# A hybrid encoder layer on one NeuronCore: input projections as products of split operands, and eight modulation sums moved to the solve stage

## The reference

```
sh1, sc1, g1, sh2, sc2, g2 = split(mod, 6)
h  = rms_norm(x, norm1) * (1 + sc1) + sh1
zp = h @ w_in                                 # 512 x 1024 by 1024 x 2824
z_rwkv, z_pool, z_fox = columns 0:1024, 1024:1280, 1280:2824 of zp
mixed = concat(rwkv7(z_rwkv), pool(z_pool), forgetting_attention(z_fox))
x  = x + g1 * (mixed @ w_out)
h  = rms_norm(x, norm2) * (1 + sc2) + sh2
x  = x + g2 * moe(h)                          # 4 of 32 experts, clamped SwiGLU
out = rms_norm(x, norm_f)
```

## Time and profile before

| | |
|---|---|
| time, median of 3 runs | 1626.63 us (1625.39 to 1629.79) |
| profiled execution: its own time, its span | 1626.56 us, 1624.6 us |
| projections, first `rw` to the end of `v` 3 and its `ada` | 38.2 to 211.8 us of the span |
| of these: `q` 3 ends, `lora` and `kkn`, `k` 0 begins, `f` ends | 124.2, to 130.7, 180.7 us |
| solve and attention (first `MP` to last `GH`) | 221.7 to 321 us |
| output projection, router | 328 to 426 us |
| experts and end | 426 us to the end |

### The profile page before, as it was taken

The page is one execution under the profiler, slowest core; times in us unless marked ns, Lnnn a source line. Parts: engine busy times, 40 slices in busy tenths (PEclk is TensorE's granted clock), DMA queues, the critical chain, the costliest instruction groups (busy, mean ns, idle before and its releaser), DMA issues.

```text
span 1624.6 us, 22048 instructions
## 1 busy us (share of the span) xinstructions
PE 1542.7 (95%) x8260; PEld 1163.2 (72%) x8260; DVE 1341.9 (83%) x1048; ACT 979.2 (60%) x787; POOL 187.9 (12%) x210
## 2 busy tenths in 40 slices
PE   3999989998699999999999999999999999999996
PEld 2444358845567787888888888888888888888873
DVE  5557447474878999999999999999999999999987
ACT  4013233311546776777777777777777777777772
POOL 1000121000001110100000100000110000010051
PEclk9999999998789999999999999999999999999998
DMA  9686020242369998999999999999999999999993
GB/s 377 254 343 236 29 91 29 69 168 110 143 258 347 339 390 335 381 388 390 388 380 383 381 380 387 396 391 376 387 379 387 386 395 385 377 388 377 375 379 123
DMA packets 85761, 506.81 MB, mean 312 GB/s; under 512 B 11008, under 2 KB 12336, under 8 KB 33360
## 3 DMA queue, kind: packets, MB, share of 16 engines
q1 hardware_dynamic: 70880, 453.85, 71.5%
q0 software_dynamic: 9104, 34.08, 5.8%
q10 hardware_dynamic: 5728, 18.18, 2.8%
HBM read 477.25 MB, written 28.84 MB: 312 GB/s over the span
## 4 chain that ended last, share of the span: by engine, by line
PE 87%; DVE 7%; DMA 2%; issue 2%; ACT 1%; POOL 1%; SPq 0%; DVEq 0%; POOLq 0%
PE ps L2067 61%; PE ps L1218 8%; PE ps L2083 2%; PE ps L1991 2%; PE ps L1295 2%; PE ps L1120 2%; PE ps L1224 2%; DVE w_lo L1474 2%; PE ps L2046 2%; DMA Wt<-in_ada_w 2%; PE ps L2056 1%; PE ps L1166 1%; PE ps L1193 1%; PE ps L1185 1%; PE ps L2089 0%
## 5 line engine op out<-in xcount | busy, mean ns | idle before, releaser
L1474 DVE TENSOR_TENSOR w_lo<-w_raw,w_hi 128x2048 fp32r<-128x2048 f32 x384 | 864.9, 2287 | 72.5 <-ACT w_hi L1468 72.4
L1468 ACT ACTIVATE w_hi<-w_raw 128x2048 fp32r<-128x2048 f32 x384 | 736.6, 1920 | 291.0 <-PE ps L2067 291.0
L2067 PE MATMUL ps<-w_hi,xTh 128*128 128x512 f32 x1024 | 408.3, 399 | 6.4 <-DVE w_lo L1474 5.8
L2067 PE MATMUL ps<-w_lo,xTh 128*128 128x512 f32 x1024 | 401.6, 392 | 0.0
L2067 PE MATMUL ps<-w_hi,xTl 128*128 128x512 f32 x1024 | 275.7, 391 | 0.0
L2067 PEld LDWEIGHTS ps<-w_hi,xTh 128*128 128x128 f32 x1024 | 194.6, 190 | 60.0 <-issue 16.5
L2067 PEld LDWEIGHTS ps<-w_hi,xTl 128*128 128x128 f32 x1024 | 193.4, 189 | 40.4
L2067 PEld LDWEIGHTS ps<-w_lo,xTh 128*128 128x128 f32 x1024 | 194.3, 190 | 38.5
L2067 PE MATMUL ps<-w_hi,aTh 128*128 128x512 f32 x512 | 202.4, 395 | 0.0
L2067 PE MATMUL ps<-w_lo,aTh 128*128 128x512 f32 x512 | 199.4, 389 | 0.0
L2067 PE MATMUL ps<-w_hi,aTl 128*128 128x512 f32 x512 | 157.6, 389 | 0.0
(11 more groups left out here) (396 smaller groups left out, 1372.3 us busy)
## 6 DMA issues: line engine op xcount, KB each, us to landing
w_raw<-in_moe_w_gu SPq DMA_DIRECT2D x256, 1024.0 KB, 6.6
w_raw<-in_moe_w_down SPq DMA_DIRECT2D x128, 1024.0 KB, 7.0
Wt<-in_ada_w SPq DMA_DIRECT2D x19, 1024.0 KB, 10.4
y_rows<-R ACTq DMA_DIRECT2D x30, 512.0 KB, 6.7
Wt<-in_w_in SPq DMA_DIRECT2D x5, 2048.0 KB, 13.4
y_rows<-Wt POOLq DMA_DIRECT2D x1, 8704.0 KB, 40.7
R<-in_ada_w SPq DMA_DIRECT2D x5, 1024.0 KB, 8.2
R<-in_x SPq DMA_DIRECT2D x2, 2048.0 KB, 10.3
```

Source lines behind the costliest of these rows:

```text
L1468: nc.scalar.activation(w_hi[:, at[-1] % HI_SLOTS, :], w_raw[:, at[-1] % RAW_SLOTS, :], ACT.Copy).then_inc(hi_rdy, 1)
L1474: nc.vector.tensor_tensor(w_lo[:, s, :], w_raw[:, s, :], w_hi[:, at[-1] % HI_SLOTS, :].bitcast(F32), ALU.subtract).then_inc(lo_rdy, 1)
L2067: ins = mm(ps[:, bank0 + c, :], x[:, k, :], w[:, 512 * (banks * i + c):512 * (banks * i + c) + 512], start=(first and i == 0 and x is xh a ...
```

## The change

The projections are computed from split operands. `hT` is split into `hTh` (rounded, ACT) and `hTl` (rest, DVE, in place of `hT`), once. The weights are split 128 columns at a time: ACT writes the rounded part of 8 x 128 columns to one of four slots `blk_hi`, DVE writes the rest in place (`blk_lo` is the memory of `blk`). A new step `sp` i does that for split i, two jobs ahead of the job that needs it; the first four are made before the steps. A projection job is then 24 float32r matmuls in place of 8 in float32. `v` 0 is computed in four parts of 128 columns, each as soon as its split is there; `v` 1 to 3 in one. `f` is padded to 128 columns by zeros.

The eight `acc` steps 8 to 15 become 16 passes of 128 x 1024, with two buffers `late_part` loaded by SP 512 KB at a time, and stand between `M` 1,1 and the last level of the solve, one after every second step; their four `ada` jobs stand behind `W` 0 to 3. Because `hTh` lies where the window sums go, POOL starts these only after `v` 3, and DVE finishes the pooled means at `trBK` 2; the `pm` jobs move behind `trBK` 3. The reload of `x` moves behind the last `ada`. The zeroing of output rows is laid out anew, and its wait on ACT moves from `GH` to `f`. Some semaphores are merged.

```diff
     for n in range(8):
-        steps += [("rw", n)] + acc(n)
-    steps += [("q", 0)] + turned(ADA_FIRST)
-    for n in range(4):
-        steps += ([("q", n)] if n else []) + acc(8 + n)
+        steps += product("rw", n) + (acc(n - 1) if n else [])
+    steps += product("q", 0) + acc(7) + product("q", 1) + turned(ADA_FIRST) + product("q", 2) + product("q", 3)
     steps += [("lora", n) for n in range(6)]
     steps += [("kkn", ct) for ct in range(CT)]
     for n in range(4):
-        steps += [("k", n)] + acc(12 + n)
+        steps += product("k", n)
     steps += [("rk", ct) for ct in range(CT)]
-    steps += [("pz", 0), ("pz", 1), ("f", 0)]
-    for t in range(TT):
-        steps += [("v", t), ("ada", ADA_FIRST + 4 + t)]
+    steps += product("pz", 0) + product("pz", 1)
+    steps += [("sp", SPLIT[("v", 0)]), ("sp", SPLIT[("v", 1)]), ("f", 0), ("sp", SPLIT[("v", 2)])]
+    steps += [("v", t) for t in range(TT)]
...
-    steps += [("trAV", t) for t in range(TT)] + [("pm", 0)] + [("trBK", t) for t in range(TT)] + [("pm", 1)]
+    steps += [("trAV", t) for t in range(TT)] + [("trBK", t) for t in range(TT)] + [("pm", 0), ("pm", 1)]
...
+    ada_at = solve.index(("W", 0))
     for n, s in enumerate(solve):
         steps.append(s)
+        if 6 <= n < 6 + 2 * 2 * KT and n % 2:
+            steps.append(("acc", KT + (n - 6) // 4, (n - 6) // 2 % 2))
+        if ada_at <= n < ada_at + 4:
+            steps.append(("ada", ADA_FIRST + 4 + n - ada_at))
...
+            job_done(pool, ("v", TT - 1))
             for ct in range(CT):
                 read_by(pool, ("pz", ct))
...
+            def high(i):
+                key, c = split_of(i)
+                if i >= SPLIT_SLOTS:
+                    job_done(act, SPLITS[i - SPLIT_SLOTS])
+                if SPLITS[i] == ("f", 0):
+                    act.wait_ge(pool_chain, pf_zero[0])
+                blk_ready(act, key)
+                s.activation(blk_hi[:, i % SPLIT_SLOTS, :, :], blk[BLK_OF[key] % 2][:, :, c:c + P], ACT.Copy
+                             ).then_inc(part_hi, 1)
+            act.wait_ge(ada1_sum, 1)
+            high(0)
+            high(1)
             act.wait_ge(modc_rdy, 1)
...
+            for k in range(KT):
+                act.wait_ge(h_act if k % 2 else h_dve, k // 2 + 1)
+                s.activation(hTh[:, k, :], hT[:, k, :], ACT.Copy).then_inc(part_hi, 1)
+            for i in range(2, AHEAD):
+                high(i)
...
+            def low(i):
+                key, c = split_of(i)
+                n = BLK_OF[key] % 2
+                dve.wait_ge(part_hi, split_count(i))
+                v.tensor_tensor(blk_lo[n][:, :, c:c + P], blk[n][:, :, c:c + P],
+                                blk_hi[:, i % SPLIT_SLOTS, :, :].bitcast(F32), ALU.subtract).then_inc(part_lo, 1)
+            low(0)
+            low(1)
+            for k in range(KT):
+                dve.wait_ge(part_hi, 2 + k + 1)
+                v.tensor_tensor(hTl[:, k, :], hT[:, k, :], hTh[:, k, :].bitcast(F32), ALU.subtract).then_inc(part_lo, 1)
+            for i in range(2, AHEAD):
+                low(i)
...
                     for k in range(KT):
                         if step == ("rw", 0):
-                            pe.wait_ge(h_act if k % 2 else h_dve, k // 2 + 1)
-                        ins = mm(b[0:rows, :], w[:, k, c:c + rows], hT[:, k, :], start=(k == 0), stop=(k == KT - 1))
+                            pe.wait_ge(part_lo, 2 + k + 1)
+                        mm(b, wh[:, k, :], hTh[:, k, :], start=(k == 0), stop=False)
+                        mm(b, wl[:, k, :], hTh[:, k, :], start=False, stop=False)
+                        ins = mm(b, wh[:, k, :], hTl[:, k, :], start=False, stop=(k == KT - 1))
                 elif kind == "v":
...
-                    for k in range(KT):
-                        ins = mm(b, hT[:, k, P * t:P * t + P], w[:, k, :], start=(k == 0), stop=(k == KT - 1))
+                    for part in (((3,), (0,), (1,), (2,)) if t == 0 else ((0, 1, 2, 3),)):
+                        lo, hi = part[0], part[-1] + 1
+                        o = b[:, P * lo:P * hi]
+                        oc = o.rearrange("p (c n) -> p c n", n=P)
+                        pe.wait_ge(part_lo, split_count(SPLIT[("v", part[-1] if t == 0 else 2)]))
+                        for k in range(KT):
+                            mm(oc, hTh[:, k, ts], blk_hi[:, lo:hi, k, :], start=(k == 0), stop=False)
+                            mm(o, hTh[:, k, ts], wl[:, k, P * lo:P * hi], start=False, stop=False)
+                            ins = mm(oc, hTl[:, k, ts], blk_hi[:, lo:hi, k, :], start=False, stop=(k == KT - 1))
```

More of the change, by code:

```diff
@@ L134 @@
 STEPS = plan()
-JOBS = [s for s in STEPS if s[0] not in ("fox", "acc")]
+JOBS = [s for s in STEPS if s[0] not in ("fox", "acc", "sp")]
 JOB = {s: n for n, s in enumerate(JOBS)}
@@ L216, in build @@
         R0 = early.enter_context(nc.sbuf_tensor("R0", [P, LATE], F32))
+        rounded = ExitStack()
+        blk_lo = [rounded.enter_context(nc.sbuf_tensor(f"blk_lo{n}", [P, KT, 512], F32R)) for n in range(2)]
+        hTh = rounded.enter_context(nc.sbuf_tensor("hTh", [P, KT, S], F32R))
+        blk_hi = rounded.enter_context(nc.sbuf_tensor("blk_hi", [P, SPLIT_SLOTS, KT, P], F32R))
+        rounded.close()
         Wt = early.enter_context(nc.sbuf_tensor("Wt", [P, 24576], F32))
@@ L339, in build @@
         late_in = [sem(f"late_in{s}") for s in range(3)]
+        late2_in = [sem(f"late2_in{s}") for s in range(2)]
         ada_acc = sem("ada_acc")
@@ L734, in _ @@
                     continue
-                if kind == "acc" or "A" not in READERS[kind]:
+                if kind == "sp":
+                    high(step[1])
+                if kind in ("acc", "sp") or "A" not in READERS[kind]:
                     continue
@@ L1004, in _ @@
                         v.tensor_tensor(Kh[:, ct, :], kT[:, ct, :], Kh[:, ct, :], ALU.mult).then_inc(elem_dve, 1)
+                if step == ("trBK", 2):
+                    for ct in range(CT):
+                        dve.wait_ge(pool_sum, ct + 1)
+                        for h in range(2):
+                            hs = slice(HD * h, HD * h + HD)
+                            tt = win[ct][h][hs, :]
+                            link(v.tensor_tensor(fix[hs, :], tt[:, PAD:2 * PAD], rcnt[hs, ct, :], ALU.mult))
+                            link(v.tensor_tensor(fix[hs, :], fix[hs, :], pz[hs, ct, PAD:2 * PAD], ALU.subtract))
+                            link(v.scalar_tensor_tensor(out=tt[:, PAD:PAD + S], in0=tt[:, PAD:PAD + S],
+                                                        scalar=1.0 / POOL_WINDOWS[2 * ct + h],
+                                                        in1=pz[hs, ct, PAD:PAD + S], op0=ALU.mult, op1=ALU.subtract))
+                            last = v.tensor_copy(tt[:, PAD:2 * PAD], fix[hs, :])
+                            if h == 0:
+                                link(last)
+                        last.then_inc(pooled, 1)
                 if "D" not in READERS[kind]:
@@ L1150, in _ @@
                 kind = step[0]
-                if kind == "acc":
+                if kind in ("acc", "sp"):
                     continue
@@ L1628, in _ @@
             s_.activation(gm, gm, ACT.Exp).then_inc(gexp_rdy, 1)
-            s_.activation(sat[:], sat[:], ACT.Sigmoid, scale=ALPHA).then_inc(sat_rdy, 1)
+            s_.activation(sat[:], sat[:], ACT.Sigmoid, scale=ALPHA).then_inc(gexp_rdy, 1)
             xt_evac(0, 0)
@@ L1662, in _ @@
             act.wait_ge(tail_mm, 1)
-            s_.activation(tailT, ps[:, 4:6, :], ACT.Copy).then_inc(tail_ev, 1)
+            s_.activation(tailT, ps[:, 4:6, :], ACT.Copy).then_inc(gmt_rdy, 1)
             sigmoid(E - 1, place(E - 1, KT - 1))
```

150 lines of the change are left out of this document (88 added, 62 removed).

## The result

The changed kernel takes 1666.5 us, the median of 4 runs (1660.09 to 1672.41), beside 1627.82 us (1625.39 to 1629.79) of the kernel before on the same chip: 1.0239 times as long, interval 1.0219 to 1.0259. I had forecast 1626.5 us, 1616 to 1637. It is slower, and outside the range.

The account below looks back on a forecast made before the run. PE was taken to bound the projections, and DVE in a loop with PE the solve. From 1626.6 us: - 14.5 (to `v` 3) + 1.5 (to `MP`) + 1.0 (restart) + 3.4 (`ada`) + 8.5 (sums) = 1626.5, range 1616 to 1637.

Parts of the forecast that it names:

- the gain of 14.5 us to the end of `v` 3: Projections: `v` 3 ends at 197.3 against 211.8, of which 3.5 us are only the `ada` jobs moved away.
- Prices: A job of 24 products 5.45 us; a split's halves 1.22 and 1.04; the 16 half sums 19.0 us of DVE.
- Start: First projection: `rw` 0 starts 4.3 us late, at 42.5, and loses 1.7 us to half clock.
- `rw` and `q`: `q` 3 ends at 115.1 instead of 124.2, 9.1 us gained; split 8 hidden, 2.0 us wait ahead of `ada`.
- `lora` to `k`: `k` 2 waits 6.3 us for split 14, then 1.7 of half clock; `k` 3 ends at 151.4, before 158.3.
- `v`: Split 22 and the parts of `v` 0 come together; `v` 0 ends at 181.0, `v` 3 at 197.3.
- To the first `MP`: From `v` 3 to `MP` 11.3 us, before 9.8: loss 1.5; DVE finishes the second mean in 2.7.
- Solve: Late sums expose 8.5 us (bounds 4 and 19); the four `ada` jobs add 3.4.
- the term of the clock: Ahead of the solve: 1.0 us (0 to 1.7) for a slower restart after PE idles some 3 us.
- the falling clock in the solve: Sign that the prediction is wrong: the clock column falls in the solve; no size given.
- a DVE that is full: Sign in the solve: DVE busy over 90% in 230 to 290 us.
- DVE becomes the bound: Rival, in the solve: all 19.0 us of late sums exposed, 1626.5 + 10.5 = 1637 us; chance 0.29.

Follow-up runs that it names:

- e3: Changed kernel with the zeroing of output rows issued after `q` 3 instead of after `rw` 7: 1654.87 us, 1.0171 of the kernel before.
- e4: Changed kernel with split 14 (for `k` 2) made ahead of `q` 3: 1651.57 us, 1.0168 of the kernel before.
- e5: Changed kernel with 41 matmuls of constants put where PE stands idle: 1660.54 us, 1.0205 of the kernel before.
- e6: Changed kernel with DVE's finish of the pooled means and the `pm` jobs behind the solve's first level: 1656.17 us, 1.0192 of the kernel before.
- e1: Kernel before, float32 projections kept, with the late sums in the solve and their four `ada` jobs at its end: 1646.99 us, ratio 1.0132.
- e2: Changed kernel without the late sums, their loads and their four `ada` jobs: 1650.13 us, 1.0127 of the kernel before.
- e9: e8 with the pooled windows moved so that POOL's sums and DVE's finish run beside the `v` products: 1617.60 us, 0.9937 of the kernel before.
- e8: Changed kernel with e3, e4, e6 and the late sums as eight whole rows in the `v` stage: 1631.75 us, 1.0020 of the kernel before.
- e10: Changed kernel with e3 and e4 together: 1649.85 us, 1.0124 of the kernel before.

## Why the prediction was wrong

The direction of each term was right: products gain, waits in the projections and sums in the solve give it back. What failed is that the gain of 14.5 us to the end of `v` 3 was nothing, and that three costs were missing or far too small: the zeroing transfer beside the loads, DVE's finish of the means ahead of the first `MP`, and the slow clock around the waits. On the marks of the table the misses add up to the whole difference: 13.7 us to the end of `v` 3 (steps 3 to 5), 6.0, 12.6 and 2.3.

1. **Prices: right.** A job of 24 products takes 5.55 us (forecast 5.45), a split's halves 1.22 and 1.05 us (1.22 and 1.04), the products of 128 columns 0.111 us at full clock (0.12). The Trainium skill's 81 ns ("TensorE: Matmul & The Clock Gate", Back-to-back issue gap) is lower than what this trace shows.
2. **Start: right.** `rw` 0 at 43.38 (42.5), half clock until 46.
3. **`rw` and `q`: failed, 8.8 us.** `q` 3 ended at 123.9, not 115.1: 0.9 from the start, 1.2 from 12 jobs of 5.55 us, 1.8 for split 8 (forecast as hidden), 3.0 because PE waited 5.0 us ahead of the `ada` jobs and not 2.0, and 1.9 because these then ran at a lower clock (5.37 us, not 3.5). I took the loads by their durations of before, and had no zeroing transfer in the sum. It ran beside the `k` block before, too (DMA share 1.01 in 110 to 124 us), but behind it in order of issue, and the block landed in 13.2 us, not 25.9. e3 shows that the zeroing makes up 5.0 of the 8.8.
4. **`lora` to `k`: right.** `k` 2 waited 5.9 us (6.3) for split 14; with the half clock behind it, it cost 6.7 us by e4 (8.0). To the start of `v` 0 another 0.9 us was lost.
5. **`v`: failed, 4.0 us.** 0.8 us of waiting for split 22, which by the sum came together with the parts, and then half clock into `v` 1. The stretch took 31.8 us in each run with split products but e5 (33.4). That the clock makes it so long is read from the table; no run removed the wait.
6. **To the first `MP`: failed, 6.0 us (17.3 instead of 11.3).** POOL's sums took 7.0 us (7.1), but I let DVE finish the first mean beside them and start the rest at their end. In the order of steps the finish stands behind the second `trBK` copy. It began 3.6 us later and did both means (5.3 us instead of 2.7). e6 gets 6.4 us back.
7. **Solve: the term of the clock, 9.9 us instead of 1.0.** The sums' exposed time was 10.2 us (8.5 forecast, and 4 to 19 as bounds); DVE needed 21.4 us for the 16 half sums (19.0), 1361 ns in place of 1260 for each of the 14 two-input passes. The stretch with the `ada` jobs grew by 5.4 us (3.4); they take 1.06 us each there, not 0.86. What I had priced far too low is the slow clock in the solve: 4.9 us more between `T` and `W` and 5.0 ahead of `T`, where I had 1.0 for one restart. The 5.0 hang on the idle time ahead of `MP`: e1, with `MP` 10.7 us behind `v` 3, has none of them, and e5, which fills the idle time, has 2.1. The 4.9 do not follow from DVE's waits one by one: behind five of them the clock was 0.98 to 1.00. Most of the 4.9 stand at the wait for POOL. The sums alone bring them (e1), and so in part does the changed kernel without the sums (e2, 2.8 us). Why that stretch is 13 us long and not 7 is open.

Of the signs that I had named, the falling clock in the solve came, and a DVE that is full did not: it was busy 43.0 of the 60 us from 230 to 290 (72%, forecast over 90%). PE's idle time came from single sums that stood ahead of a normalisation, not from a lack of DVE time.

The rival "DVE becomes the bound" names DVE's part of this and allows for slow clock behind stalls, but its price, 10.5 us, was that of the sums alone. And its 1637 still had the 14.5 us of gain in it, of which nothing arrived.

Left open: the 2.3 us at the end, where the code is the same and the other kernels differ by up to 6 us (1296.3 to 1302.5), and why the clock differs between executions of the same kernel.

## What to carry to other kernels

When PE gets faster, everything that was hidden behind it is priced again: for each step, list the transfers and the other engines' blocks that fall in the same window, those that the change doesn't touch too (before, PE had no wait behind the zeroing; after, it cost 5 us). Put a term for the clock beside each new wait of PE, with a wide range: here it went from nothing to several times the wait. Read the clock stretch by stretch before you say which wait it belongs to. Work that an engine has to do once belongs where that engine idles and its inputs are ready: the same sums cost 15 us between `T` and `W` (e1) and next to nothing beside `v` (e9), where DVE had had over 20 us to spare, once memory had been found for them.

## What the runs showed of the hardware

- In the changed kernel 12 of the 14 two-input passes of the late sums took DVE 1.27 us, and two that began during a product of POOL took 1.59 and 2.17. Which began first mattered: four passes that began just ahead of such a product kept their 1.27 us, and the product took 1.7 to 2.1 us in place of 1.26. In e9 both engines' rows stretch each other. The timeline of DVE and then of POOL: two low halves took 3.51 us where the same two took 2.36 in e8, and POOL's sums 1.9 to 2.0 us instead of 1.06.

```profile
162.81 3.51 DVE L956 TENSOR_TENSOR blk_lo<-Wt,blk_hi 128x1024 fp32r<-128x1024 f32 x2 [0.50 <-ACT blk_hi L766]
```

```profile
161.32 1.91 POOL L680 TENSOR_TENSOR Wt<-R 128x527 f32<-128x527 f32 x1 [38.97 <-DVE Wt L1121]
...
167.32 1.06 POOL L681 TENSOR_TENSOR R<-Wt 128x525 f32<-128x525 f32 x1
```

  The Trainium skill ("GPSIMD Engine Reference", Specifications) has the two sharing SBUF interfaces where a DVE instruction has two inputs there; both rows agree.
- An idle time of 0.8 us in `v` 0 was followed by over 6 us at half clock: the granted clock was 0.50 in each stretch from 191 to 196 us, 0.81 in the next and then 1.00. After 5.4 us of idle time at the start it was half for 2.7 us of work. In e10 a wait of the same 0.8 us ahead of `k` 3 (at 142.8 us) was followed by clock 1.00; Around that wait PE had products of 512 columns, and ahead of the one in `v` 0 products of 128. The length of a wait says little about what it costs.
- An 8704 KB transfer of POOL's queue, issued 4.8 us ahead of it, stretched a 2048 KB load from 9.7 to 25.9 us; before, with the transfer issued 1.3 us behind it, such a load took 13.2.
